# Sample states loaded ahead of the second output weights, sample rows' products and turns placed elsewhere, and the first weight block in two transfers

## The chip, the cores and the metric

One NeuronCore of a Trainium2 chip runs the kernel. The metric is device microseconds of one execution. Before the change the median of three runs is 1743.33 us (1741.56 to 1744.11).

## The reference

One step of a one-layer decoder runs for a prompt (512 rows of width 1024) and a sample group (8 sequences of 4 new rows, so 32 rows), with the same weights:

```python
h = rmsnorm(x);  hq|hf|hi|hg|mq|mk|mv = h @ w_in          # 7 blocks of 512 columns
HGRN2 (4 heads of 128): S_t = diag(f_t) S_{t-1} + k_t i_t^T;  o_t = S_t^T q_t
MoBA (8 heads of 64): attention over blocks of keys
x += concat(HGRN2 out, MoBA out) @ w_out                  # halves o0, o1
x += cross_attention(rmsnorm(x)) @ w_xo                   # queries: w_xq, halves xq0, xq1
x += hierarchical_moe(rmsnorm(x))                         # 2 of 32 experts for each row
y = rmsnorm(x)
```

The sample group starts from `state_hgrn` (8 x 4 states of 128 x 128, 2 MB) and reads paged keys and values; its new states are an output.

## The kernel before, in words

All data is f32. The rows stand in five tiles: tiles 0 to 3 of 128 prompt rows, and tile 4 (`NT`) of the 32 sample rows. Each engine has its own program, written in order by hand; they meet at semaphores.

Weights come in blocks of 1024 x 512 (2 MB), sent by SyncE (`weights`, line 612) into two slots in turn. A block goes only when the product that last reads the slot's earlier block is done (`last`, line 568). SyncE's program is one list (from line 640): the key pages and value pages of the sample batches (`key_pages(b)`, `value_pages(b)`, four transfers of 256 KB each), `o1` (line 643), the memory values, `xq0` to `xo1` (line 663), then the expert weights (lines 672 and 676 wait before the first of these). POOL has a queue of its own: constants, the sample states (line 757, into the tile `r_x`), their write-back after the update (line 763), the reload of x into the same place (line 766) and the memory keys.

Products are put in a ring of seven PSUM banks in the order of `plan_jobs` (line 122). A job names the engine that empties its bank (A is ScalarE, V is VectorE), and each engine must take its jobs in this order. TensorE waits for a bank through `J.wait_free`, for a copy through `J.wait_emptied`.

The steps that matter, in order of time:

- **Start.** Each tile is normed (ScalarE squares and roots at lines 839 and 841, VectorE scales at line 1299), turned by TensorE (`turn`, line 1961) and multiplied by block `mk` (`key_rows`, line 2025, products at line 2001). For a prompt tile a product is a loop over 8 blocks of 128 rows of the weights, two passes each.
- **Sample states.** After the last value product of the prompt (line 2139), TensorE waits at line 2182 for the states, multiplies by them (lines 2185 and 2188) and makes the updates (line 2198); VectorE adds them (line 1562).
- **Output projection.** `rows_summed(half, i)` is tile i by `o0` or `o1`. These products stand between the turning of the sample keys and the sample scores. For tile 4 the product is 64 small passes for each half (`quarters`, line 1974). VectorE adds the result to x (`add_rows`, line 1606, and line 1610 for tile 4).
- **Second norm and turn.** When both halves of a tile are added, ScalarE takes its root (`cross_norm_root`), VectorE scales it (`cross_norm`) and TensorE turns it (`cross_turn`). `X1_HALF` (line 115) is the order of the tiles. Tile 4 needs the sample outputs turned (`out_turned(1)`, copied by VectorE).
- **Queries.** `features_out("xq", half)` (line 1978) first multiplies the sample rows (line 1974), then makes four chunks of 128 features for all prompt rows (line 1989) and turns the sample rows' result (line 1992).

Then come cross-attention, its output, the router and the experts, whose 384 MB of weights pass through the same memory.

Of the kernel before, what the change touches and what calls it, by code (L numbers as in the profile page):

```python
# [28 lines left out]
KC = D // P  # L29
SEQ = 512  # L30
NT = SEQ // P
# [80 lines left out]


LAST_HALF = [NT] + list(range(NT))
X1_HALF = [0, 1, NT, 2, 3]

BANKS = (0, 1, 2, 3, 4, 5, 7)
RING = len(BANKS)
# [3 lines left out]
def plan_jobs():  # L122
# [3 lines left out]
    def add(eng, *name):  # L126
        jobs.append((name, eng))

    def turned(what, tiles):
        for i, _ in tiles:  # L130
            add("A", what, i, 0)
            add("V", what, i, 1)
# [85 lines left out]
    add("A", "Os", 1)  # L218
    turned("h2T", [(0, 0)])
    add("V", "OsT", 1)  # L220
    add("V", "x1", 0, NT)
    add("V", "x1", 1, NT)
    turned("h2T", [(1, 0)])
    add("V", "x1", 1, 2)
    turned("h2T", [(NT, 0)])
    add("V", "x1", 1, 3)
    turned("h2T", [(2, 0)])
    turned("h2T", [(3, 0)])

    def summed(what, turn, samples):  # L230
# [17 lines left out]
        for name in logit[NT:]:  # L248
            add("V", *name)

    for half in range(2):
        add("A", "xq", half, "rows")
        for c in range(5):
            add("AV"[c % 2], "xq", half, c)
    for h in range(XH + 1):
        if h < XH:
            for i in range(2):
# [79 lines left out]
def step_kernel(nc, a):  # L337

    with ExitStack() as ctx:
# [3 lines left out]
        def sem(name):  # L343
            return ctx.enter_context(nc.semaphore(name))
# [156 lines left out]
        const_in = sem("const_in")  # L501
        ident_in = sem("ident_in")
        w_in = [sem(f"wslot{n}_in") for n in range(2)]
        mem_in = sem("mem_in")
        s0_in = sem("s0_in")
        k_in = [sem(f"k{n}_in") for n in range(3)]
# [57 lines left out]
        def tok(i):  # L564
            return slice(P * i, P * i + rows(i))
# [2 lines left out]
        last = {"hf": ("hf", 4), "hq": ("hq", 4), "mk": ("mk", 4), "mq": ("mq", 4), "mv": ("mv", 4),  # L568
                "hi": ("hi", 4), "hg": ("hg", 4)}
        for n in range(2):  # L570
            last[f"o{n}"] = ("x1", n, (NT, LAST_HALF[-1])[n])
            last[f"xk{n}"] = ("mem", n, 1)
            last[f"xv{n}"] = ("mem", 2 + n, 1)
            last[f"xq{n}"] = ("xq", n, 4)
            last[f"xo{n}"] = ("x2", n, (NT, LAST_HALF[-1])[n])
# [30 lines left out]
        def _(sp):  # L606
# [5 lines left out]
            def weights(tag):  # L612
                n = WPOS[tag]
                name, col, _ = WBLOCKS[n]
                if n >= 2:
                    J.wait_filled(sp, *last[WBLOCKS[n - 2][2]])
                src = a[name][0].rearrange("(k p) n -> p k n", p=P)[:, :, 512 * col:512 * (col + 1)]
                sp.dma_start(wslot[n % 2], src).then_inc(w_in[n % 2], 16)

            def value_pages(*batches):  # L620
                for b in batches:
                    load_pages(sp, pages, vbuf[b % 4], "cache_moba_v", b, v_in)
# [6 lines left out]
            def key_pages(b):  # L629
                load_pages(sp, pages, kbuf[b % 3], "cache_moba_k", b, k_in[b % 3])  # L630
# [9 lines left out]
            sp.wait_ge(qx_done, 1)  # L640
            J.wait_filled(sp, "S", MB - 1, NT - 1)
            key_pages(1)
            weights("o1")
            value_pages(3)
            J.wait_filled(sp, "OT", 3)
            sp.wait_ge(out_mv, 32)
            key_pages(2)
            sp.wait_ge(out_memk[1], 16)
            value_pages(2)
            J.wait_filled(sp, "KT", 0, 3)  # L650
# [5 lines left out]
            for b in (5, 6, 7):  # L656
                J.wait_filled(sp, "KT", b - 3, 3)
                key_pages(b)
            J.wait_filled(sp, "Os", 0)
            value_pages(4, 5, 6, 7)  # L660
            J.wait_filled(sp, "Os", 1)
# [171 lines left out]
        def _(act):  # L833
# [24 lines left out]
            def turned(what, i):  # L858
                evac(hT[:, 0:4, tok(i)], what, i, 0,
                     view=lambda s: s.rearrange("p (k t) -> p k t", k=4)[:, :, 0:rows(i)])  # L860
# [244 lines left out]
                J.wait_filled(act, "h2T", X1_HALF[n - 2], 1)  # L1105
                cross_norm_root(n)
            turned("h2T", X1_HALF[3])
            turned("h2T", X1_HALF[4])

            def scaled_q(half, c):  # L1110
                J.wait_filled(act, "xq", half, c)
# [5 lines left out]
                                         s[:, 0:128].rearrange("p (c t) -> p c t", c=4), ACT.Copy, scale=XD ** -0.5)  # L1117
                J.empties(ins, "xq", half, c)

            for half in range(2):  # L1120
                sample_rows("xq", half)
                for c in (0, 2, 4):
                    scaled_q(half, c)

            for h in range(XH + 1):
                if h < XH:
# [148 lines left out]
        def _(dve):  # L1275
# [395 lines left out]
            turned("h2T", 0)  # L1671
            cross_norm(1)
            out_turned(1)
            add_rows("x1", 0, NT)
            add_rows("x1", 1, NT)
            turned("h2T", 1)
            cross_norm(2)
            add_rows("x1", 1, 2)
            turned("h2T", NT)
            cross_norm(3)  # L1680
            add_rows("x1", 1, 3)
            turned("h2T", 2)
            cross_norm(4)
            turned("h2T", 3)
            for half in range(2):
                for c in (1, 3):
                    J.wait_filled(dve, "xq", half, c)
                    J.empties(dve.tensor_scalar(qT[:, 4 * half + c, 0:SEQ], J.bank("xq", half, c), XD ** -0.5, None,
                                                ALU.mult), "xq", half, c)

            for h in range(XH + 1):
                if h < XH:
# [258 lines left out]
        def _(pe):  # L1951
# [23 lines left out]
                                        start=(k == 0), stop=(k == KC - 1), skip_group_check=True)  # L1975
                return ins

            def features_out(what, *key, chunks=range(5)):

                w = weights(what if not key else f"xq{key[0]}")  # L1980
                for c in chunks:
                    if c == 0:
                        J.wait_free(pe, what, *key, "rows")
                        J.fills(quarters(J.bank(what, *key, "rows"), NT, w, hT), what, *key, "rows")
                    J.wait_free(pe, what, *key, c)
                    s = J.bank(what, *key, c)
                    if c < 4:
                        for k in range(KC):
                            ins = pe.matmul(s, w[:, k, P * c:P * (c + 1)], hT[:, k, 0:SEQ], start=(k == 0), stop=(k == KC - 1))  # L1989
                    else:  # L1990
                        J.wait_emptied(pe, what, *key, "rows")
                        ins = pe.transpose(s[:, 0:P], srows[:, :], ident[:, :])
                    J.fills(ins, what, *key, c)

            def rows_of(name, i, w, lhs):
                J.wait_free(pe, *name)
                if i == NT:
                    J.fills(quarters(J.bank(*name), i, w, lhs), *name)
                    return
                for k in range(KC):  # L2000
                    ins = pe.matmul(J.bank(*name), lhs[:, k, tok(i)], w[:, k, :], start=(k == 0), stop=(k == KC - 1))  # L2001
                J.fills(ins, *name)

# [21 lines left out]
            def key_rows(i):  # L2025
                J.wait_emptied(pe, "hT", i, 0)
                J.wait_emptied(pe, "hT", i, 1)
                if i == 0:
                    weights("mk")
                rows_of(("mk", i), i, w, hT)  # L2030

            for i, r in TILES:
# [267 lines left out]
            sample_out(1)  # L2300
            cross_turn(0)
            out_turned(1)
            J.wait_emptied(pe, "hgT", NT)
            J.wait_emptied(pe, "OsT", 1)
            rows_summed(0, NT)
            rows_summed(1, NT)
            cross_turn(1)
            rows_summed(1, 2)
            cross_turn(2)
            rows_summed(1, 3)  # L2310
            cross_turn(3)
            cross_turn(4)

            def summed(what, wtag, lhs, turned, n0, meanwhile, samples, logit=None):

# [17 lines left out]
                if logit:  # L2333
                    logit(NT)

            J.wait_emptied(pe, "h2T", X1_HALF[-1], 0)
            J.wait_emptied(pe, "h2T", X1_HALF[-1], 1)
            for half in range(2):
                features_out("xq", half)

            for c in range(5):
                J.wait_emptied(pe, "xq", 1, c)
# [245 lines left out]
```

## Time and profile before

| | us |
|---|---|
| median of three runs | 1743.33 |
| the profiled execution | 1745.59 |
| its span, first to last instruction | 1743.4 |
| TensorE busy in it | 1453.9 (83%) |
| VectorE busy | 503.1 (29%) |
| ScalarE busy | 271.9 (16%) |
| DMA, mean rate | 299 GB/s |

A busy share is a mean over stages with different limits. To value a change in one stage one reads there which engine stood still, for how long, and what ended the wait. The chain that ended last is followed back from the last instruction, each step to what released it. In a timeline, the bracket at the end of a line is the idle time of the engine just before it and what ended it.

### The profile page before, as it was taken

How to read it: one execution, taken by the hardware profiler on the slowest of the kernel's cores; microseconds unless marked ns; L12 is line 12 of the kernel's file. 1: busy time of each engine (PE TensorE's matmuls, PEld its weight loads, DVE VectorE, ACT ScalarE, POOL GpSimd, SP SyncE). 2: the span in 40 equal slices, each digit the busy share in tenths (PEclk: the TensorE clock that was granted, in tenths of full speed). 3: DMA queues.
4: the chain of work that ended last, by engine and by line, in shares of the span. 5: the costliest groups of instructions: out<-in, count | busy, mean ns of one | idle time of the engine just before them, and what ended most of it. 6: DMA issues, size and time to landing. Idle time of an engine off the chain costs nothing.

```text
span 1743.4 us, 17609 instructions
## 1 busy us (share of the span) xinstructions
PE 1453.9 (83%) x6988; PEld 644.6 (37%) x6988; DVE 503.1 (29%) x929; ACT 271.9 (16%) x594; POOL 96.9 (6%) x108
## 2 busy tenths in 40 slices
PE   6999999879989999869778877877887788788781
PEld 3444554444454564523222322322232223223220
DVE  2056775453230331432121211112121211112124
ACT  3114234432210220200000000000000000000002
POOL 3100000000000000000000000000000000000002
PEclk9999999989989999979989989988998998899895
DMA  8931220476361256459999999999999999999974
GB/s 298 278 122 48 77 95 15 156 267 237 121 254 49 72 218 246 160 224 428 427 427 427 430 427 428 428 427 427 428 429 426 428 426 428 428 428 428 422 315 175
DMA packets 76085, 521.99 MB, mean 299 GB/s; under 512 B 8466, under 2 KB 9026, under 8 KB 51456
## 3 DMA queue, kind: packets, MB, share of 16 engines
q1 hardware_dynamic: 58112, 468.47, 65.4%
q0 software_dynamic: 14800, 45.98, 7.9%
q10 hardware_dynamic: 3120, 6.82, 1.0%
q8 instruction: 36, 0.59, 0.1%
q14 instruction: 17, 0.14, 0.0%
HBM read 496.98 MB, written 32.11 MB: 303 GB/s over the span
## 4 chain that ended last, share of the span: by engine, by line
PE 48%; DMA 40%; DVE 7%; ACT 2%; issue 2%; SPq 1%; POOL 0%; POOLq 0%; ACTq 0%; DVEq 0%
DMA ring<-w 39%; PE psum L2533 12%; PE psum L2001 10%; PE psum L1989 7%; PE psum L2091 3%; PE psum L2510 3%; PE psum L1974 1%; PE psum L2218 1%; PE psum L2366 1%; PE psum L2389 1%; DVE ring L1417 1%; PE psum L2351 1%; DMA ring<-w_in 1%; PE psum L2206 1%; PE psum L1961 1%
## 5 line engine op out<-in xcount | busy, mean ns | idle before, releaser
L2510 PE MATMUL psum<-ring,r_c 128*64 128x512 f32 x1536 | 368.9, 636 | 84.6 <-DMA ring<-w 83.7
L2533 PE MATMUL psum<-ring,r_c 128*64 128x512 f32 x1024 | 260.8, 663 | 90.3 <-DMA ring<-w 78.6
L2510 PEld LDWEIGHTS psum<-ring,r_c 128*64 128x64 f32 x1536 | 120.1, 147 | 329.9 <-issue 212.1
L1904 DVE TENSOR_SCALAR r_c<-r_c 128x512 f32<-128x512 f32 x32 | 13.7, 427 | 751.3 <-ACT r_c L1208 751.3
L2533 PEld LDWEIGHTS psum<-ring,r_c 128*64 128x64 f32 x1024 | 82.4, 151 | 246.5 <-issue 204.0
L1989 PE MATMUL psum<-r_h,ring 128*128 128x512 f32 x320 | 138.8, 594 | 0.0
L2001 PE MATMUL psum<-ring,r_h 128*128 128x512 f32 x256 | 114.6, 607 | 4.6 <-DMA ring<-w_in 4.6
L1906 DVE RECIPROCAL r_c<-r_c 128x512 f32<-128x512 f32 x32 | 107.3, 3353 | 1.1
L1208 ACT ACTIVATE r_c<-psum 128x512 f32<-128x512 f32 x32 | 19.1, 597 | 540.4 <-PE psum L2510 540.4
L1989 PEld LDWEIGHTS psum<-r_h,ring 128*128 128x128 f32 x320 | 60.6, 191 | 75.3 <-issue 75.3
L809 POOL DMA_INDIRECT out_rows<-r_c,maskd x32 | 31.6, 988 | 897.7 <-ACT r_c L1218 865.4
L2001 PEld LDWEIGHTS psum<-ring,r_h 128*128 128x128 f32 x256 | 49.3, 195 | 65.0 <-issue 64.7
L1218 ACT ACTIVATE r_c<-psum 128x512 f32<-128x512 f32 x32 | 19.1, 597 | 334.2 <-PE psum L2533 334.2
L2510 PE MATMUL psum<-r_h,r_c 128*64 128x512 f32 x256 | 57.6, 592 | 0.0
L2510 PE MATMUL psum<-r_mix,r_c 128*64 128x512 f32 x256 | 57.6, 592 | 0.0
L2091 PE MATMUL psum<-ring,r_h 128*128 128x512 f32 x128 | 57.0, 598 | 0.6 <-DVE r_x L1470 0.6
L2001 PE MATMUL psum<-ring,r_mix 128*128 128x512 f32 x128 | 56.8, 597 | 0.9 <-ACT r_mix L852 0.9
L2001 PE MATMUL psum<-ring,r_c 128*128 128x512 f32 x128 | 56.1, 595 | 0.0
L1606 DVE TENSOR_TENSOR r_x<-r_x,psum 128x512 f32<-128x512 f32 x16 | 11.0, 687 | 95.5 <-PE psum L2001 83.7
L852 ACT ACTIVATE ring<-psum 128x512 f32<-128x512 f32 (+3 forms) x63 | 28.0, 531 | 64.8 <-PE psum L2001 26.1
L2091 PEld LDWEIGHTS psum<-ring,r_h 128*128 128x128 f32 x128 | 23.7, 190 | 31.0 <-issue 30.7
L2001 PEld LDWEIGHTS psum<-ring,r_c 128*128 128x128 f32 x128 | 23.9, 190 | 29.3 <-issue 29.3
(350 smaller groups left out, 1295.4 us busy)
## 6 DMA issues: line engine op xcount, KB each, us to landing
ring<-w SPq DMA_DIRECT2D x160, 2048.0 KB, 22.2
r_h<-w SPq DMA_DIRECT2D x16, 2048.0 KB, 28.2
r_mix<-w SPq DMA_DIRECT2D x16, 2048.0 KB, 29.9
ring<-w_in SPq DMA_DIRECT2D x7, 2048.0 KB, 14.1
out_rows<-zeros POOLq DMA_DIRECT2D x3, 4096.0 KB, 21.6
ring<-cache_mem_v SPq DMA_DIRECT2D x8, 1024.0 KB, 9.4
ring<-cache_mem_k POOLq DMA_DIRECT2D x8, 1024.0 KB, 7.7
ring<-cache_moba_v SPq DMA_DIRECT2D x24, 256.0 KB, 7.1
```

The costliest lines, as they stand in the source:

```text
L809: pool.indirect_dma_start(half_rows, bass.IndirectOffsetOnAxis(ap=sidx[:, e:e + 1], axis=0), ys[e % 2], None, bounds_check=2 * NE * CAP - ...
L852: J.empties(act.activation(out, view(src) if view else src, ACT.Copy), *name)
L1208: act.activation(he[u], psum[2 + 2 * u], ACT.Exp, scale=-1.0).then_inc(up_exp, 1)
L1218: act.activation(ys[u], psum[7], ACT.Copy).then_inc(y_free, 1)
L1417: v(dve.reciprocal(g, g))
L1906: dve.reciprocal(he[u], he[u]).then_inc(dve_moe, 1)
L1961: ins = pe.transpose(s[:, P * k:P * k + r], src[0:r, P * (4 * half + k):P * (4 * half + k + 1)], ident[0:r, 0:r])
L1989: ins = pe.matmul(s, w[:, k, P * c:P * (c + 1)], hT[:, k, 0:SEQ], start=(k == 0), stop=(k == KC - 1))
L2001: ins = pe.matmul(J.bank(*name), lhs[:, k, tok(i)], w[:, k, :], start=(k == 0), stop=(k == KC - 1))
L2091: ins = pe.matmul(J.bank("mem", n, i), memT[:, k, P * i:P * (i + 1)], w[:, k, :], start=(k == 0), stop=(k == KC - 1))
L2510: ins = pe.matmul(psum[2 + 2 * u + m][CAP * half:CAP * (half + 1), :], xT[:, k, CAP * u:CAP * (u + 1)], moe_place(2 * q + m, u)[:, kk, 512 ...
L2533: ins = pe.matmul(psum[7][CAP * half:CAP * (half + 1), :], heT[u][:, k % 4, CAP * (k // 4):CAP * (k // 4 + 1)], moe_place(4 + q, u)[:, kk, ...
```

## The change

First block: `mk` is sent as two transfers, of its first and last four row blocks. The first product waits for the first alone, and for the second before its fifth row block.

Loads: `o1` moves from behind the key pages of batch 1 to behind those of batch 6. The value pages of batch 3 move behind the key pages of batch 2, and SyncE waits for the sample states before it sends them.

Rows: tile 4 becomes the last of `X1_HALF`. The product of tile 2 by `o1` and the turn of tile 1 go ahead of tile 4's product by `o0`, that of tile 3 behind it, and tile 4's product by `o1` goes between the turns of tiles 2 and 3. Tile 4's turn goes behind the second chunk of the first query block, and its query product from the head of this block to just ahead of the fourth chunk. The other engines' lists follow the same order.

```diff
-X1_HALF = [0, 1, NT, 2, 3]
+X1_HALF = [0, 1, 2, 3, NT]
...
-            last[f"o{n}"] = ("x1", n, (NT, LAST_HALF[-1])[n])
+            last[f"o{n}"] = ("x1", n, NT)
...
+                if tag == "mk":
+                    sp.dma_start(wslot[n % 2][:, 0:KC // 2, :], src[:, 0:KC // 2, :]).then_inc(w_first_in, 16)
+                    sp.dma_start(wslot[n % 2][:, KC // 2:, :], src[:, KC // 2:, :]).then_inc(w_in[n % 2], 16)
+                    return
...
             key_pages(1)
-            weights("o1")
-            value_pages(3)
             J.wait_filled(sp, "OT", 3)
             sp.wait_ge(out_mv, 32)
             key_pages(2)
+            sp.wait_ge(s0_in, 16)
+            value_pages(3)
...
                 key_pages(b)
+                if b == 6:
+                    weights("o1")
...
+            scaled_q(0, 0)
+            turned("h2T", NT)
+            scaled_q(0, 2)
+            sample_rows("xq", 0)
+            scaled_q(0, 4)
+            sample_rows("xq", 1)
+            for c in (0, 2, 4):
+                scaled_q(1, c)
...
-            add_rows("x1", 0, NT)
-            add_rows("x1", 1, NT)
+            add_rows("x1", 1, 2)
             turned("h2T", 1)
             cross_norm(2)
-            add_rows("x1", 1, 2)
-            turned("h2T", NT)
-            cross_norm(3)
+            add_rows("x1", 0, NT)
             add_rows("x1", 1, 3)
             turned("h2T", 2)
+            cross_norm(3)
+            add_rows("x1", 1, NT)
+            turned("h2T", 3)
             cross_norm(4)
-            turned("h2T", 3)
...
+                    if half == 0 and c == 1:
+                        turned("h2T", NT)
...
+                    if name == ("mk", 0) and k == KC // 2:
+                        weights("mk")
...
                 if i == 0:
-                    weights("mk")
+                    pe.wait_ge(w_first_in, 16)
...
+            rows_summed(1, 2)
+            cross_turn(1)
             J.wait_emptied(pe, "hgT", NT)
             J.wait_emptied(pe, "OsT", 1)
             rows_summed(0, NT)
+            rows_summed(1, 3)
+            cross_turn(2)
             rows_summed(1, NT)
-            cross_turn(1)
-            rows_summed(1, 2)
-            cross_turn(2)
-            rows_summed(1, 3)
             cross_turn(3)
-            cross_turn(4)
...
-            for half in range(2):
-                features_out("xq", half)
+            features_out("xq", 0, chunks=(0, 1), rows_at=None)
+            cross_turn(4)
+            features_out("xq", 0, chunks=(2,), rows_at=None)
+            J.wait_emptied(pe, "h2T", NT, 0)
+            J.wait_emptied(pe, "h2T", NT, 1)
+            features_out("xq", 0, chunks=(3, 4), rows_at=3)
+            features_out("xq", 1)
```

## Rows read from the trace of the kernel before

**Rows 1.** The page's chain that ended last, by engine and by line.

```profile
PE 48%; DMA 40%; DVE 7%; ACT 2%; issue 2%; SPq 1%; POOL 0%; POOLq 0%; ACTq 0%; DVEq 0%
DMA ring<-w 39%; PE psum L2533 12%; PE psum L2001 10%; PE psum L1989 7%; PE psum L2091 3%; PE psum L2510 3%; PE psum L1974 1%; PE psum L2218 1%; PE psum L2366 1%; PE psum L2389 1%; DVE ring L1417 1%; PE psum L2351 1%; DMA ring<-w_in 1%; PE psum L2206 1%; PE psum L1961 1%
```

**Rows 2.** A wait of SyncE's queue: total us, times, longest us.

```profile
SPq L672 <- PE psum L2407: 18.4, 1, 18.4
```

**Rows 3.** Timeline of the start, TensorE: start us, us, engine, line.

```profile
17.84 8.53 PE L2001 MATMUL psum<-ring,r_h 128*128 128x512 f32 x16 [4.58 <-DMA ring<-w_in]
```

**Rows 4.** Timeline around the sample states: SyncE's and POOL's issues, then TensorE.

```profile
363.42 0.40 SPq L618 DMA_DIRECT2D ring<-w_out  x1
373.57 1.88 SPq L603 DMA_DIRECT2D ring<-cache_moba_k  x4
...
366.62 1.74 POOL L757 DMA_DIRECT2D r_x<-state_hgrn  x1 [296.37 <-PE psum L2154]
...
371.03 2.37 PE L2139 MATMUL psum<-ring 128*64 128x512 f32 x16 [1.89 <-ACT ring L852]
383.04 0.77 PE L2185 MATMUL psum<-ring,atts 128*128 128x128 f32 x2 [9.63 <-issue]
```

**Rows 5.** End of the projection: chain, TensorE, and stretches (length, busy times, PEclk, DMA, GB/s).

```profile
486.14 3.51 issue
...
515.74 1.97 PE L1961 MATMUL psum<-ident,r_c 128*128 128x128 f32 x8 [3.28 <-DVE r_c L1299]
550.04 1.95 PE L1974 MATMUL psum<-ring,r_h 128*32 128x128 f32 x64
...
489.60:496.00 6.40, 6.35 (x129) 6.19 (x129) 1.13 (x4) 0.00 (x0) 0.00 (x0) 0.56 1.02 412
518.50:522.20 3.70, 3.67 (x65) 3.31 (x65) 0.00 (x0) 0.00 (x0) 0.00 (x0) 0.50 0.42 162
```

**Rows 6.** SyncE's DMA queue in 0:12, 12:15, 15:18: packets, MB, share.

```profile
q1 hardware_dynamic: 1009, 3.25, 81.2%
...
q1 hardware_dynamic: 563, 1.15, 104.5%
...
q1 hardware_dynamic: 359, 0.70, 64.4%
```

**Rows 7.** POOL's DMA queue in 371:372, then 374:378; the states' landing (us).

```profile
q0 software_dynamic: 7, 0.03, 7.0%
...
q0 software_dynamic: 222, 0.91, 66.8%
...
r_x<-state_hgrn POOLq DMA_DIRECT2D x1, 2048.0 KB, 16.3
```

**Rows 8.** Timeline: reload of x (VectorE), keys 6 (SyncE), first product by o1 (TensorE).

```profile
409.25 0.69 DVE L1606 TENSOR_TENSOR r_x<-r_x,psum 128x512 f32<-128x512 f32 x1 [11.76 <-DMA r_x<-x_prompt]
...
422.67 1.88 SPq L603 DMA_DIRECT2D r_h<-cache_moba_k  x4
...
465.47 7.13 PE L2001 MATMUL psum<-ring,r_mix 128*128 128x512 f32 x16
```

**Rows 9.** Timeline of VectorE and ScalarE: sample rows' add, tile 3's norm, a turn emptied.

```profile
493.35 1.17 DVE L1610 TENSOR_TENSOR r_x<-r_x,psum 32x128 f32<-32x128 f32 x4 [3.80 <-PE psum L1974]
511.62 0.69 DVE L1606 TENSOR_TENSOR r_x<-r_x,psum 128x512 f32<-128x512 f32 x1 [3.61 <-PE psum L2001]
514.40 1.28 DVE L1299 SCALAR_TENSOR_TENSOR r_c<-r_x,nt,gain 128x1024 f32<-128x1024 f32 x1
...
512.40 1.06 ACT L839 ACTIVATE r_c<-r_x 128x1024 f32<-128x1024 f32 x1 [6.12 <-DVE r_x L1606]
516.89 0.60 ACT L852 ACTIVATE r_h<-psum 128x512 f32<-128x512 f32 x1 [2.62 <-PE psum L1961]
```

**Rows 10.** Issue and landing of the query weights (two transfers), SyncE.

```profile
493.34 18.64 SPq L618 DMA_DIRECT2D ring<-w_xq  x2
...
DMA to landing us min/median/max: 8.1/12.0/15.8
```

More of the change, by code:

```diff
@@ L220, in plan_jobs @@
     add("V", "OsT", 1)
+    add("V", "x1", 1, 2)
+    turned("h2T", [(1, 0)])
     add("V", "x1", 0, NT)
[L222 to L225, printed above, removed]
     add("V", "x1", 1, 3)
     turned("h2T", [(2, 0)])
+    add("V", "x1", 1, NT)
     turned("h2T", [(3, 0)])
@@ L249, in summed @@
             add("V", *name)
-    for half in range(2):
-        add("A", "xq", half, "rows")
-        for c in range(5):
-            add("AV"[c % 2], "xq", half, c)
+    add("A", "xq", 0, 0)
+    add("V", "xq", 0, 1)
+    turned("h2T", [(NT, 0)])
+    add("A", "xq", 0, 2)
+    add("A", "xq", 0, "rows")
+    add("V", "xq", 0, 3)
+    add("A", "xq", 0, 4)
+    add("A", "xq", 1, "rows")
+    for c in range(5):
+        add("AV"[c % 2], "xq", 1, c)
     for h in range(XH + 1):
@@ L503, in step_kernel @@
         w_in = [sem(f"wslot{n}_in") for n in range(2)]
+        w_first_in = sem("first_half_of_mk_in")
         mem_in = sem("mem_in")
@@ L1107, in _ @@
             turned("h2T", X1_HALF[3])
-            turned("h2T", X1_HALF[4])
             def scaled_q(half, c):
@@ L1118, in scaled_q @@
                 J.empties(ins, "xq", half, c)
[L1120 to L1123, printed above, removed]
+            scaled_q(0, 0)
[6 more added lines that the diff above has]
+                scaled_q(1, c)
             for h in range(XH + 1):
@@ L1976, in quarters, with features_out @@
                 return ins
-            def features_out(what, *key, chunks=range(5)):
+            def features_out(what, *key, chunks=range(5), rows_at=0):
                 w = weights(what if not key else f"xq{key[0]}")
                 for c in chunks:
-                    if c == 0:
+                    if c == rows_at:
                         J.wait_free(pe, what, *key, "rows")
@@ L2334, in summed @@
                     logit(NT)
-            J.wait_emptied(pe, "h2T", X1_HALF[-1], 0)
-            J.wait_emptied(pe, "h2T", X1_HALF[-1], 1)
-            for half in range(2):
-                features_out("xq", half)
+            J.wait_emptied(pe, "h2T", NT - 1, 0)
+            J.wait_emptied(pe, "h2T", NT - 1, 1)
+            features_out("xq", 0, chunks=(0, 1), rows_at=None)
[5 more added lines that the diff above has]
+            features_out("xq", 1)
             for c in range(5):
```

## The prediction

> **What bounds the kernel now.** I read the chain that ended last first. TensorE holds 48% of the span and DMA 40%, nearly all of the latter expert weights [rows 1]. So there are two halves: up to about 760 us a chain of TensorE products, and after it a stream of expert weights. All that the change touches lies in the first half. What is saved there reaches the end if the stream's start follows the chain: SyncE waits 18.4 us for the products at line 2407 before it sends the first expert weights (line 672) [rows 2]. It is a queue that waits for slots, so an earlier chain starts it earlier. I count a us before 660 as a us at the end.
>
> In the first half I looked for places where TensorE stands still on the chain. Three lie in the change's path: 4.58 us before the first product, which waits for the block mk [rows 3]; 9.63 us at 373.4 to 383.0, which the chain calls issue, but the next instruction reads r_x and line 2182 waits for the sample states [rows 4]; and the end of the first output projection, with idle stretches of 3.51 and 3.28 us and slow products behind both: the granted clock is 0.56 (mostly the 1.2 GHz level) at 489.6 to 496 and 0.50 at 518.5 to 522.2 [rows 5].
>
> **Part 1: block mk in two transfers.** Nothing is removed; SyncE issues one transfer more (about 0.4 us of its time) and the first product waits for 1.05 MB instead of 2.10 MB. Ahead of mk in its queue lie four prompt tiles, a gain and the sample rows, 2.75 MB together. The queue had moved 3.25 MB by 12 us, so 0.50 MB of mk, and 1.15 MB more from 12 to 15 us [rows 6], 0.383 MB a us. The first half has passed at 12 + 0.55 / 0.383 = 13.4. The full block has passed at about 16.9 (0.45 MB after 15 at the 0.23 MB a us left beside the constants, 0.70 MB in 3 us [rows 6]), and its product began at 17.84, so 0.9 later; the first then begins at 14.3 to 14.5. Gain 3.4 us. Half of the first tile's sixteen passes takes 4.3 us, so the second half, due at 17.9, is there when wanted. Bounds: all of the 4.58 us, or 1.5 us if the second transfer's packets mix with the first's. The loads behind it keep their order, and block hf moves already while mk's products run. The tiles that follow are TensorE work without a gap, so the gain stays.
>
> What speaks against it: here the queue moves block mk at 0.383 MB a us, with six smaller transfers ahead of it. The Trainium skill (DMA: Bandwidth & Descriptors, Bandwidth) gives 6.15 us for 1 MB alone and asks for batches of at least 1 MiB; two such in a row would take 12.3 us, land the second half near 23 us, and make this gain about zero.
>
> **Part 2: the states ahead of o1.** Before, SyncE issues o1 (2.10 MB, 363.42) and behind it value pages (1.05 MB) just ahead of the states' transfer on POOL (366.62) [rows 4]. In 371 to 372 the states' queue q0 has moved only 7 packets [rows 7]: it got nothing until the 3.15 MB before it had passed. Then the key pages of 373.57 took part of the rest: from 374 to 378 q0 moved 0.91 MB with 66.8% of the engines' time [rows 7]. The states landed after 16.3 us [rows 7].
>
> After, only the key pages of batch 1 precede, which SyncE sends before o1, and they are through. Scaled to all engines, q0's rate is 0.91 / 4 / 0.668 = 0.34 MB a us. From the end of the POOL instruction (366.62 + 1.74 = 368.4) 2.10 MB take 6.2 us; the 0.26 MB of hg_prompt that ACT sends meanwhile add 0.8; the key pages of 373.57 come in for the last us. I take TensorE's start as 376.2. Its own ready time is 371.03 + 2.37 = 373.4 [rows 4]. Gain 383.04 - 376.2 = 6.8 us. Bounds: 9.6 (landing hidden), and 2.3, where q0 starts as late as before (371.5) and moves at 0.23 MB a us as it did beside q1 (9.2 us, landing 380.7).
>
> By the fit of the Trainium skill (DMA: Bandwidth & Descriptors, Anatomy of one DMA), 2.0 us and bytes at 436 GB/s, the states would land after an estimated 6.8 us, at 373.4: the gain would be 9.6 and the sum 20.3.
>
> What the added wait holds up: behind SyncE's wait for the states stand the value pages 3 and 2 and the keys 3 to 7. The first 12 issues take 5.6 us of SyncE (1.88 for four [rows 4]), and keys 3 are wanted after tile 1's product of the output projection. The backlog of value pages shares the engines with the states' write-back and the reload of x, whose first part VectorE awaits at 409.25 (11.76 us idle [rows 8]); a later landing costs VectorE first, and TensorE needs what follows it only behind a further 7 us product. I cost it at nothing; without that cover it is the delay itself, an estimated 1 to 3 us for 1.05 MB more at 0.34 MB a us. o1 is now sent behind keys 6, which went at 422.67, and is wanted at 465.47 [rows 8]: 41 us of cover for 3 MB. Its cost is nothing.
>
> **Part 3: sample rows moved.** After the turn of the sample outputs ends at 486.14, TensorE waited for VectorE's copies (3.51 us) and did both sample products at the low clock, 6.4 us [rows 5]. In the new order it goes on with tile 2: product 7.03, turn of tile 1 1.0, sample product of the first half 1.95 (the price at the high clock [rows 5]), product of tile 3 7.03: at 503.1. The copies are done long before. Now the chain is tile 3's norm: from the start of its add at 511.62 to the end of its scaling, 514.40 + 1.28, is 4.1 us in the old order [rows 9]; so it ends at 507.3. TensorE fills 1.0 (turn of tile 2) and 1.95 (second sample product) and then waits a little over 1 us. VectorE then adds the sample rows, 1.17; ACT does their square and root, about 1.4 (its square alone 1.06), and only then empties tile 3's turn, 0.60 [rows 9]. So the query products start at 507.3 + 1.2 + 1.4 + 0.6 = 510.5. What is late next is that ACT norm.
>
> Before, these products began at 522.2, with the sample rows' product (3.67 at the low clock) done. Now that product and the turn of the sample rows (0.7) fall inside the query stage at the high clock: 1.95 + 0.7. I also charge 1.7 us of low clock behind the new gap, as behind the old one (3.67 against 1.95 [rows 5]). Gain 522.2 - 510.5 - 2.65 - 1.7 = 7.3 us. Bounds: 9.0 if the clock stays up, 4.0 if the query weights come late: they are now released by the first sample product at 496.1 instead of 493.3, and before they landed after 15.8 us [rows 10], at 509.1. The engines were full of memory keys and values then, so I expect the same landing; at worst 511.9, with as much again lost to the clock.
>
> **Sum.** 3.4 + 6.8 + 7.3 = 17.5 us. The profiled execution took 1745.6 us (span 1743.4 and 2.2 around it), 2.3 above the median of the runs, 1743.3; taking the 17.5 off its own time gives 1728.1, and off the median 1725.8, which is my forecast. The bounds together give 7.8 to 23.2, so 1720 to 1735.5.
>
> **Rivals.**
> - The states' transfer is slow by itself (its rows are 512 bytes long). For it: q0 moved no more than 0.23 MB a us in this stretch; against it: it had q1 and hg_prompt beside it. 368.4 + 9.2 and 1.7 for the same company give a landing at 379.3, a gain of 3.7, a total of 1728.9. Chance 0.15.
> - Covers hold better: the states land before TensorE is ready, and the clock stays up. By the idle time in the rows: 3.4 + 9.6 + 9.0 = 22.0, total 1721.3. For it: before, the states had o1 ahead of them. Against: q0's measured rate. Chance 0.10. The fit of the Trainium skill (DMA: Bandwidth & Descriptors, Anatomy of one DMA) would act like this.
> - A weight block comes late: either mk's halves mix or slow each other (gain 0 of 3.4), or the query weights land 2.8 later (3.3 lost). Total 1729.1. For it: q1 and q0 share the engines then; against: both were limited by total bandwidth. Chance 0.08. [...]
> - Nothing reaches the end: the expert stream keeps its own start. Total 1743.3. Against: the wait of [rows 2], for a product of the chain. Chance 0.04.
> - Slower: o1 becomes the wait at its first product. It is now sent about 41 us before it is due [rows 8], and nothing is sent ahead in its place. Each us beyond 41 from issue to landing is a us of waiting; past 41 + 17.5 = 58.5 us the kernel is slower, and at 64 us the total is 1743.3 - 17.5 + 23 = 1749. Against: the query weights, with 6 MB beside them, needed 15.8 us [rows 10]. Chance 0.03.
>
> **How the numbers follow.** The forecast holds 0.60. Three other faster cases hold 0.33 and lie at 1721 to 1729. The range 1719 to 1733.5 takes these with their bounds; the far end of the sum of all low bounds and the last two rivals are left out. About 0.2% (3.5 us) is what a measurement can tell from no change: faster by more than that 0.93, within it 0.04, slower 0.03.
>
> **What would show it.** In the changed profile: the first product near 14.5; states landing in 8 to 10 us and idle time ahead of line 2185 of under 4 us; no idle stretch before the sample products, whose time is half; a short gap before tile 3's turn, and the first query product about 12 us earlier than the earlier gains alone put it; expert weights sent 17 us sooner. The forecast is wrong if the states' transfer still takes over 12 us, if line 2001 waits for the second half of mk, or if the query products wait for their weights.

## The result, and the profile after

The changed kernel takes 1729.38 us (median of 4 runs, 1724.6 to 1730.4), the kernel before 1743.72 (4 runs beside it, 1741.56 to 1744.43): a ratio of 0.9914, 95% interval 0.9893 to 0.9935, so 14.3 us less. The forecast was 1725.8 with a range of 1719 to 1733.5. One execution of a run further down (tile 3's turn emptied first) took 2980.56 us and is left out of its ratio. The profiled executions differ by 15.1 us (spans of 1743.4 and 1728.3). Their timelines can be laid side by side and say where the time went:

| place on TensorE | before | after | earlier by | of it new, and forecast |
|---|---|---|---|---|
| start of the first product | 17.84 | 14.39 | 3.45 | |
| start of the second product | 27.08 | 24.29 | 2.79 | |
| product of values ahead of the states | 371.03 | 368.42 | 2.61 | part 1: 2.6 (3.4) |
| first product with the states | 383.04 | 375.60 | 7.44 | |
| first product of the output projection | 399.39 | 391.62 | 7.77 | part 2: 5.2 (6.8) |
| first scores after the queries | 580.73 | 565.19 | 15.54 | part 3: 7.8 (7.3) |
| first expert product | 760.97 | 745.43 | 15.54 | |
| end of the span | 1743.4 | 1728.3 | 15.1 | sum: 15.5 (17.5) |

SyncE's wait ahead of the first expert weights is as long as before (18.4 us in [rows 2]), and their first transfers go out 15.55 us earlier, so the stream of expert weights did start with the chain and kept the gain. The wait in the changed kernel, then SyncE's issue in the kernel before and in the changed one:

```profile
SPq L684 <- PE psum L2429: 18.5, 1, 18.5
...
659.79 2.29 SPq L672 DMA_DIRECT2D ring<-w  x4
...
644.24 2.14 SPq L684 DMA_DIRECT2D ring<-w  x4
```

**The start.** The timeline of the changed kernel's TensorE, against [rows 3]: start us, us, engine, line, in brackets the idle time ahead and what ended it.

```profile
14.39 9.19 PE L2019 MATMUL psum<-ring,r_h 128*128 128x512 f32 x16 [1.04 <-DMA ring<-w_in]
...
24.29 7.03 PE L2019 MATMUL psum<-ring,r_h 128*128 128x512 f32 x16
```

The idle stretch is 1.04 us instead of 4.58. The product itself takes 9.19 us instead of 8.53, so 0.7 of the 3.45 is gone before the second product. That is a difference between these two executions and no price of the split (Part 1 further down). Its weight loads show how (the same timeline, TensorE's weight loads): the first come 0.85 us apart, the later ones 0.43, half as far.

```profile
16.23 0.34 PEld L2019 LDWEIGHTS psum<-ring,r_h 128*128 128x128 f32 x1 [0.52 <-issue]
17.09 0.34 PEld L2019 LDWEIGHTS psum<-ring,r_h 128*128 128x128 f32 x1 [0.52 <-issue]
...
19.12 0.19 PEld L2019 LDWEIGHTS psum<-ring,r_h 128*128 128x128 f32 x1 [0.24 <-issue]
19.55 0.19 PEld L2019 LDWEIGHTS psum<-ring,r_h 128*128 128x128 f32 x1 [0.24 <-issue]
```

**The states.** POOL's issue, its landing (the list of DMA issues) and TensorE's timeline, against [rows 4] and [rows 7]:

```profile
363.99 1.74 POOL L769 DMA_DIRECT2D r_x<-state_hgrn  x1 [291.48 <-PE psum L2172]
...
r_x<-state_hgrn POOLq DMA_DIRECT2D x1, 2048.0 KB, 11.5
...
368.42 2.37 PE L2157 MATMUL psum<-ring 128*64 128x512 f32 x16 [1.90 <-ACT ring L864]
375.60 0.77 PE L2203 MATMUL psum<-ring,atts 128*128 128x128 f32 x2 [4.81 <-issue]
```

The landing takes 11.5 us instead of 16.3, and the idle stretch ahead of the product is 4.81 instead of 9.63. The queues say what is left of it. In 366 to 368, 368 to 372 and 372 to 374 (packets, MB, share of 16 engines):

```profile
q0 software_dynamic: 45, 0.18, 57.6%
q10 hardware_dynamic: 343, 0.17, 29.8%
...
q0 software_dynamic: 299, 1.22, 101.1%
...
q0 software_dynamic: 142, 0.58, 102.8%
```

POOL's queue begins about 2.8 us after the issue, as ACT's hg_prompt (q10) ends, and then moves 1.22 MB in 4 us and 0.58 MB in 2 us, 0.29 to 0.31 MB a us, with the engines full and nothing beside it. The granted clock (the third number from the end of each row) falls in the gap and stays at 0.50, the 1.2 GHz level, for the 4 us behind it:

```profile
374.00:376.00 2.00, 0.40 (x2) 0.43 (x2) 2.00 (x4) 0.00 (x0) 0.00 (x0) 0.50 1.00 346
376.00:378.00 2.00, 2.00 (x34) 1.65 (x37) 0.11 (x1) 0.00 (x0) 0.00 (x0) 0.50 1.05 387
378.00:380.00 2.00, 2.00 (x43) 1.51 (x32) 0.00 (x0) 0.00 (x0) 0.00 (x0) 0.50 1.06 387
```

**The sample rows.** TensorE's timeline from the first sample product on, then ScalarE's, and the stretch 502 to 510, against [rows 5] and [rows 9]:

```profile
485.97 1.95 PE L1990 MATMUL psum<-ring,r_mix 128*32 128x128 f32 x64
...
495.79 1.95 PE L1990 MATMUL psum<-ring,r_mix 128*32 128x128 f32 x64
499.15 1.09 PE L1977 MATMUL psum<-ident,r_c 128*128 128x128 f32 x8 [1.40 <-DVE r_c L1314]
502.18 15.70 PE L2005 MATMUL psum<-r_h,ring 128*128 128x512 f32 x32 [1.93 <-ACT r_h L864]
...
500.26 1.05 ACT L851 ACTIVATE r_c<-r_x 32x1024 f32<-32x1024 f32 x1 [2.59 <-PE psum L1977]
...
501.55 0.57 ACT L864 ACTIVATE r_h<-psum 128x512 f32<-128x512 f32 x1
...
502.00:510.00 8.00, 7.82 (x15) 3.36 (x16) 1.43 (x3) 0.12 (x1) 0.55 (x1) 0.79 0.62 224
```

The gaps of 3.51 and 3.28 us and the two sample products at the low clock are gone. In their place stand 1.40 us for tile 3's norm and 1.93 us for ScalarE, which squares the sample rows (500.26) before it empties tile 3's turn (501.55). Behind that the granted clock is 0.79 on average for 8 us: the first two query chunks take 15.70 us.

### The profile page after: what moved, and what is told of

It is laid out like the page before. It is cut to its first block, busy times and chain, and to the rows that moved or that the text cites. A ratio compares the mean times of both kernels' runs of the same rounds, so it can differ in the third digit from the quotient of the medians.

```text
span 1728.3 us, 17613 instructions
## 1 busy us (share of the span) xinstructions
PE 1451.4 (84%) x6988; PEld 638.0 (37%) x6988; DVE 502.8 (29%) x929; ACT 272.3 (16%) x594; POOL 97.3 (6%) x108
## 4 chain that ended last, share of the span: by engine, by line
PE 48%; DMA 40%; DVE 7%; ACT 2%; issue 1%; SPq 1%; POOL 0%; POOLq 0%; ACTq 0%; DVEq 0%
DMA ring<-w 39%; PE psum L2555 12%; PE psum L2019 10%; PE psum L2005 7%; PE psum L2109 3%; PE psum L2532 3%; PE psum L1990 1%; PE psum L2236 1%; PE psum L2388 1%; PE psum L2411 1%; DVE ring L1432 1%; PE psum L2373 1%; PE psum L1977 1%; PE psum L2157 1%; PE psum L2399 1%
```

## The experiments

A single run can't carry differences of 2 us here: executions of the kernel before lay between 1741.4 and 1752.6 on one chip, with granted clocks of 0.929 to 0.919. So each run is read by its trace first, at the place that its edit touches, and by its ratio second.

**One part at a time.** The kernel before, with one of the three parts each. Block mk in two transfers:

```diff
+                if tag == "mk":
+                    sp.dma_start(wslot[n % 2][:, 0:KC // 2, :], src[:, 0:KC // 2, :]).then_inc(w_first_in, 16)
+                    sp.dma_start(wslot[n % 2][:, KC // 2:, :], src[:, KC // 2:, :]).then_inc(w_in[n % 2], 16)
+                    return
...
```

> The kernel before, with the first weight block in two transfers and nothing else. Theory (three parts that add up): the first product begins at 14.4 us instead of 17.84, the second at 24.3 instead of 27.1, everything behind it 2.8 us earlier up to the wait for the sample states, the total 2.8 us below the kernel before. Rival (the later stages take it back, since the loads behind block mk or the states' transfer keep their own times): the total moves by under 1 us, and the idle time ahead of the product by the states grows by 2 to 3 us.

Measured: ratio 0.996 (0.9943 to 0.9977). The first product's row of its timeline:

```profile
14.45 9.28 PE L2008 MATMUL psum<-ring,r_h 128*128 128x512 f32 x16 [1.07 <-DMA ring<-w_in]
```

The second product begins at 24.44 instead of 27.08, 2.6 us earlier: part 1 as in the whole change. The idle stretch at the states stays (10.16 us). This trace doesn't show the lead any further on: its execution ran at a mean granted clock of 0.922, and the product of values ahead of the states came at 371.71, before at 371.03. That the lead reaches the end rests on the ratio and on the whole change.

The order of the loads:

```diff
-            weights("o1")
-            value_pages(3)
             J.wait_filled(sp, "OT", 3)
             sp.wait_ge(out_mv, 32)
             key_pages(2)
+            sp.wait_ge(s0_in, 16)
+            value_pages(3)
...
+                if b == 6:
+                    weights("o1")
```

> The kernel before, with the order of SyncE's loads changed alone (o1 behind the key pages of batch 6, the value pages of batch 3 behind a wait for the states). Theory: the states land 11 to 12 us after their issue instead of 16.3, the idle time ahead of the product by the states falls from 9.63 to 4.8 us, the total by 5 us. Rival (the loads put later cost something where they land): the states land as early, but VectorE waits longer for the reloaded rows of x and TensorE for its copies, and the total falls by 3 us or less.

Measured: ratio 0.9956 (0.994 to 0.9971). TensorE's timeline and the landing:

```profile
379.66 0.77 PE L2187 MATMUL psum<-ring,atts 128*128 128x128 f32 x2 [4.82 <-issue]
...
r_x<-state_hgrn POOLq DMA_DIRECT2D x1, 2048.0 KB, 11.5
```

The idle stretch and the landing are those of the whole change, to 0.01 us: part 2 owes nothing to the others.

The sample rows (the order on VectorE and TensorE; ScalarE's list goes with them):

```diff
             out_turned(1)
-            add_rows("x1", 0, NT)
-            add_rows("x1", 1, NT)
+            add_rows("x1", 1, 2)
             turned("h2T", 1)
...
+            rows_summed(1, 2)
+            cross_turn(1)
             J.wait_emptied(pe, "hgT", NT)
...
```

> The kernel before, with the sample rows' products and turns moved alone. Theory: no idle stretch of 3.5 us ahead of the sample products, each of which takes 1.95 us instead of 3.2; the query stage ends 7.7 us earlier, and so does the kernel. Rival (the moved products only fill time that the clock gives back in any order): the stretch of idle and low clock reappears ahead of the query products, and the total falls by 4 us or less.

Measured: ratio 0.9962 (0.9943 to 0.9981). Its first sample product and its first query chunks:

```profile
494.58 1.95 PE L1983 MATMUL psum<-ring,r_mix 128*32 128x128 f32 x64
...
510.78 16.77 PE L1998 MATMUL psum<-r_h,ring 128*128 128x512 f32 x32 [1.93 <-ACT r_h L857]
```

From the product with the states to the scores it takes 191.0 us, before 197.7: 6.7 us saved, and its two chunks took 1.07 us more than those of the whole change behind the same wait of 1.93, which makes up the difference to 7.8. By the traces the parts add up: 2.6 + 5.2 + 6.7 is 14.5. The three ratios would add to 1.2%, 21 us, with an uncertainty of about 3 us each; the interval of the split alone, 4 to 10 us, doesn't even hold its 2.6. I go by the traces, since executions differ by so much; why the ratios add to more isn't shown.

**Which of the loads held the states up?** Only o1 moved (the value pages wait for the product that o1 waited for, so that they go at the time they went):

```diff
-            weights("o1")
+            J.wait_filled(sp, *last["xv1"])
             value_pages(3)
...
+                if b == 6:
+                    weights("o1")
```

> The kernel before, with o1 alone moved behind the key pages of batch 6; the value pages of batch 3 stay where they were (with the wait for the last memory value product, which o1's own issue held before) and SyncE does not wait for the states. Theory A (the states wait for what was sent before them, 3.15 MB, of which o1 is two thirds, and then move at their own rate of 0.29 MB a us): the states' first packets come at 369 us, they share the engines with key pages and value pages only at the end, the idle time ahead of the product by the states is 5 to 6 us and the total falls by 4 to 5 us, nearly all that the second part gives. Theory B (the value pages, sent beside the states, take as much of the engines as o1 did): idle 7 us or more, the total falls by 1 to 2.5 us.

and only the value pages moved, with o1 in its old place:

```diff
             weights("o1")
-            value_pages(3)
...
+            sp.wait_ge(s0_in, 16)
+            value_pages(3)
```

> The kernel before, with o1 in its old place; only the value pages of batch 3 move behind a wait for the states. Theory A (the states wait until what was sent before them has passed, and o1's 2.1 MB are most of that): from the states' issue to the product that reads them 14.5 to 16 us (16.4 before, 11.6 in the changed kernel, 12.6 with o1 alone moved). Theory B (the pages that share the engines with the states cost most): 12 to 13 us.

POOL's issue and the product with the states, in the first of the two and in the second:

```profile
372.90 1.74 POOL L759 DMA_DIRECT2D r_x<-state_hgrn  x1 [301.61 <-PE psum L2156]
...
385.52 0.77 PE L2187 MATMUL psum<-ring,atts 128*128 128x128 f32 x2 [4.84 <-issue]
```

```profile
364.70 1.74 POOL L758 DMA_DIRECT2D r_x<-state_hgrn  x1 [293.78 <-PE psum L2155]
...
378.79 0.76 PE L2186 MATMUL psum<-ring,atts 128*128 128x128 f32 x2 [7.29 <-issue]
```

From issue to product: 16.4 us before, 12.6 with o1 moved (ratio 0.9962, 0.9946 to 0.9979), 14.1 with the pages moved (one run, 1738.08), 11.6 with both. So o1 alone takes 3.8 of the 4.8 us off and the pages alone 2.3; together they are worth less than the two added. The first is on Theory A's side; with the pages moved, 14.1 lies between the two theories' ranges, so the pages count for more than Theory A had them. The product ahead of the gap ran slower in the first of them (3.36 us instead of 2.37), so its idle stretch of 4.84 flatters it by 1.

**Is the rest of the landing the transfer's own?** The changed kernel with the states sent by SyncE instead of POOL:

```diff
             key_pages(1)
+            J.wait_filled(sp, "o", NT - 1)
+            J.wait_emptied(sp, "U", NCH - 1)
+            sp.dma_start(s0, a["state_hgrn"][0].rearrange("b h k v -> k b h v")).then_inc(s0_in, 16)
...
-            pool.dma_start(s0, a["state_hgrn"][0].rearrange("b h k v -> k b h v")).then_inc(s0_in, 16)
```

> The changed kernel, with the states' transfer sent by SyncE at the same point instead of by POOL. Theory R (rows of 512 bytes limit the transfer to 0.29 MB a us, whoever sends it): the rate stays at 0.28 to 0.30 MB a us, the landing comes 9 to 10.5 us after the issue instead of 11.5, because the first packet comes sooner, and the idle time ahead of the product falls from 4.8 to 2.8 to 3.8 us. Theory S (POOL's software queue limits it): 0.38 to 0.40 MB a us, landing after 7 to 8 us, idle time under 1.5 us.

Measured: ratio 0.9901 (0.9876 to 0.9927), and the product later after the issue, 12.8 us instead of 11.6:

```profile
363.79 0.89 SPq L655 DMA_DIRECT2D r_x<-state_hgrn  x1
...
376.59 0.77 PE L2205 MATMUL psum<-ring,atts 128*128 128x128 f32 x2 [5.79 <-issue]
```

Neither theory, as written: the edit had moved something else. POOL's next transfer, 0.5 MB of the cross norm's gain, no longer stood behind the states on POOL's queue and went ahead of them. The gain's first bytes came at about 365.2, the states' at about 366.9, though SyncE had issued the states 0.2 us earlier. The queues in 366 to 368:

```profile
q0 software_dynamic: 96, 0.34, 64.6%
q1 hardware_dynamic: 49, 0.10, 15.2%
```

So once more, with that gain held until the states are there:

```diff
+            pool.wait_ge(s0_in, 16)
             pool.dma_start(gain[:, :], a["g_cross"].to_broadcast([P, D])).then_inc(gain_in, 16)
```

> The changed kernel with the states sent by SyncE's queue, and GpSimd's load of the cross norm's gain held until they have landed, so that nothing new goes ahead of them. Theory S (it was the gain that held the states up when SyncE sent them: issue 363.8, first packets about 367, product 12.8 us after the issue): the states' bytes begin to move by 366.5, their product comes 9.5 to 11 us after the issue, and the idle stretch ahead of it is 2 to 4 us instead of 4.81; the time 1 to 3 us below the changed kernel's, ratio to the kernel before about 0.990. Theory R (2 MB in rows of this length take about 11.5 us beside the key loads whoever sends them): 11.5 us or more, idle stretch 4.5 to 6, ratio as the changed kernel's.

Measured: ratio 0.9913 (0.9893 to 0.9932). SyncE's issue, TensorE's timeline, and SyncE's queue in 365 to 367:

```profile
362.93 0.88 SPq L655 DMA_DIRECT2D r_x<-state_hgrn  x1
...
367.56 3.35 PE L2160 MATMUL psum<-ring 128*64 128x512 f32 x16 [1.89 <-ACT ring L867]
...
373.06 0.76 PE L2206 MATMUL psum<-ring,atts 128*128 128x128 f32 x2 [2.15 <-issue]
...
q1 hardware_dynamic: 272, 0.56, 95.4%
```

Theory S holds: the bytes move from about 364.6 (1.7 us after the issue), the product comes 10.1 us after the issue, and the idle stretch is 2.15 us. The rate is 0.28 MB a us over these two, about as on POOL's queue: that part hardly depends on the sender. Why it is below the 0.383 of block mk [rows 6] no run here separates; rows of 512 bytes are one reading. Still the run is no faster than the changed kernel. The product ahead of the gap took 3.35 us instead of 2.37, and more of what follows the gap ran at the low clock: from the start of that product to the first product of the output projection it is 22.11 us, in the changed kernel 391.62 - 368.42 = 23.20 (and 24.36 in its second profile, below, where the product ahead of the gap was as slow). Of 2.66 us of idle time 1.1 reached the chain against the first of these profiles and 2.25 against the second, too little for a ratio to show.

**What stands behind the wait of 1.93 us?** The changed kernel with ScalarE emptying tile 3's turn ahead of the sample rows' norm:

```diff
+                if n == 4:
+                    turned("h2T", X1_HALF[3])
...
-            turned("h2T", X1_HALF[3])
```

> The changed kernel, with ScalarE emptying tile 3's turn ahead of the sample rows' square and root instead of behind them. Theory (that norm of the sample rows is what the first query product waits for): the query products start 1.2 us sooner after tile 3's turn (idle 0.8 instead of 1.93), and if the shorter stop keeps the clock up, their first two chunks take 13.9 instead of 15.7 us: 1.2 to 3 us in all. Rival (VectorE's add and copy, or the query weights, land as late): idle time above 1.6 us, nothing gained.

Measured: ratio 0.9881 (0.9855 to 0.9907; three executions). The wait falls to 1.30 us and has a new cause, the query weights:

```profile
506.85 13.97 PE L2006 MATMUL psum<-r_h,ring 128*128 128x512 f32 x32 [1.30 <-DMA ring<-w_xq]
```

From the first sample product to the scores it is 76.85 us, in the changed kernel 79.22. Of these 2.4 us 0.63 are the wait; the chunks' 1.73 are the clock, and the run with the states first had chunks of 14.00 us behind the full wait of 1.93. So 1.7 of the 2.4 aren't this edit's for certain. Both edits so far together (SyncE's states, gain not held):

> The changed kernel with both edits (states sent by SyncE, tile 3's turn emptied first). Theory: the two gains add up, 2 to 5 us below the changed kernel, so 1725 us less 2 to 5 on a chip where the changed kernel takes its 14 us less than the kernel before. Rival (one stop is replaced by the next on the same chain): 1 us or less.

Measured: ratio 0.9912 (0.9892 to 0.9932), 6.05 us idle at the states, 1.44 on the query weights and chunks of 15.37: no gain that can be measured. Then the query weights ahead of the memory values on SyncE:

```diff
-            mem_values(range(3))
-            for tag in ("xq0", "xq1", "xo0", "xo1"):
+            for tag in ("xq0", "xq1"):
+                weights(tag)
+            mem_values(range(3))
+            for tag in ("xo0", "xo1"):
```

> The changed kernel with ScalarE emptying the third tile's turn ahead of the sample rows' norm (the run before that did this had a wait of 1.30 us on the query weights ahead of the query products, and 13.97 us for the first two chunks), and with SyncE sending the two blocks of query weights ahead of the three loads of memory values (3 MB). Theory A (the query weights land late because 3 MB of memory values go ahead of them on the same queue): the weights land before the last turn is emptied, the wait ahead of the query products is named by an engine's copy and is 0.7 to 1.0 us, the first two chunks take 13.9 to 14.5 us, and the stage is 0.3 to 0.6 us shorter than in that run, 2.5 to 3 us shorter than in the changed kernel. Theory B (the 3 MB of memory keys on GpSimd's queue hold them as much): the wait is still named by the weights and is 1.2 us or more. Either way the memory values, sent later, are not waited for. Ratio to the kernel before 0.989 to 0.991.

Measured: ratio 0.9903 (0.9888 to 0.9918). SyncE's issue and the query products:

```profile
489.09 10.16 SPq L628 DMA_DIRECT2D ring<-w_xq  x2
...
502.13 13.97 PE L2008 MATMUL psum<-r_h,ring 128*128 128x512 f32 x32 [0.83 <-ACT r_h L866]
```

Theory A holds: the weights land after about 8 us instead of 11, the wait is a copy's again, 0.83 us, and from the first sample product to the scores it is 76.39 us, 2.8 less than in the changed kernel, 0.5 less than with ScalarE's edit alone. The memory values are not waited for.

**All of it together**, the states by SyncE with the gain behind them and the two edits at the query products:

> All of it together: the states by SyncE with the gain behind them, the third tile's turn first, the query weights ahead of the memory values. If both theories named first hold, the gains add: 1 to 3 us at the states and 2.5 to 3 us at the query products, ratio to the kernel before 0.987 to 0.989, faster than the changed kernel by about 4 us. If the states' product is not earlier (Theory R), about 2.5 us, 0.989 to 0.990. If the clock gives it back, 0.991.

Measured: 1725.55 us (median of 5 runs), ratio 0.9885 (0.9867 to 0.9903). TensorE's timeline at the start, at the states and at the queries:

```profile
14.48 7.11 PE L2025 MATMUL psum<-ring,r_h 128*128 128x512 f32 x16 [1.42 <-DMA ring<-w_in]
...
371.77 0.77 PE L2209 MATMUL psum<-ring,atts 128*128 128x128 f32 x2 [2.09 <-issue]
...
497.94 13.97 PE L2011 MATMUL psum<-r_h,ring 128*128 128x512 f32 x32 [0.83 <-ACT r_h L869]
```

Both gains stand in one trace: 1.1 us at the states (22.09 over the same stretch, against the changed kernel's first profile) and 2.8 at the queries (76.39). The first product at 7.11 us, which no edit touched, gave this execution 2 us more. It is also the one product that waited for the second half of mk: its weight loads, 0.43 us apart, are held up by 0.33 us at the fifth row block.

```profile
17.13 0.19 PEld L2025 LDWEIGHTS psum<-ring,r_h 128*128 128x128 f32 x1 [0.24 <-issue]
17.89 0.30 PEld L2025 LDWEIGHTS psum<-ring,r_h 128*128 128x128 f32 x2 [0.57 <-DMA ring<-w_in]
```

The changed kernel, run again to weigh those 2 us:

> The changed kernel once more, unchanged, with more runs than the four it was judged by. Two readings of the run of everything together (ratio 0.9885, with the first product at 7.11 us and the first two query chunks at 13.97): if its 4 us over the changed kernel are its own, this run gives 0.990 to 0.993 and a median of 1728 to 1732; if they are mostly the granted clock of those executions, this run may come to 0.988 to 0.990 as well. The first product of its profiled execution takes anything from 8.5 to 10.2 us, and the first two query chunks 14.0 or 15.4 to 15.7 behind the same wait of 1.93 us: the stretch from the first sample product to the scores is 77.5 or 79.2 us, by the clock alone.

Measured: 1729.7 us (median of 4), ratio 0.9906 (0.9889 to 0.9922), 16.5 us below the kernel before beside it, with the wait of 1.93 and chunks of 15.70 us again. The version with everything is the best of all by its median, 4 us below the changed kernel's, and 3.9 by the two stretches. The two intervals still overlap, and 1.7 of those us are query chunks at the high clock: they took 13.97 in all three runs with a wait of 1.30 us or less, and 15.70 in three with 1.93 (16.77 and 14.00 in two others).

## Why the prediction was right, and where it was off

The direction, the three places and the range held. Two of the signs named ahead did not come: the states landed after 11.5 us, not 8 to 10, and the idle time ahead of their product was 4.81 us, not under 4. The forecast was 3.6 us too low: 2.0 from the three terms (17.5 forecast, 15.5 in the chain), 0.4 given back in the expert stream (15.1 at the end), 0.8 between these two executions and the medians (14.3), and 0.4 because the kernel before came out at 1743.7 beside it, not at 1743.3.

- **Part 1, 3.4 forecast, 2.6 between the two profiles.** The landing was right: first product forecast for 14.3 to 14.5, measured 14.39. In the changed kernel no pass waited for the second half; in the one execution that made its first passes at full pace, it held them up by 0.33 us, at 17.89, where the forecast had it due. Assumed without saying so was that the product keeps its 8.53 us. Its first passes go at half pace for a number that differs from execution to execution: 8.52 to 10.15 us in eight of the nine traces with the split, 7.11 in the ninth, 8.53 to 9.96 in the five without. The profile before is the quickest of those five, so its pair shows too little: the second product begins at 24.05 on average in the nine, at 27.88 in the five, 3.8 us earlier. The 3.4 was not too much. The Trainium skill (DMA: Bandwidth & Descriptors, Bandwidth) gives 6.15 us for 1 MB; an estimated 12.3 us for two in a row would have made this gain zero. The trace disagrees, with 3.5 us less to wait. The Trainium skill's batch size of at least 1 MiB (the same section) is no ground against the split: half a block is 1.05 MB and meets it.
- **Part 2, 6.8 forecast, 5.2 measured.** The cause was right: o1 and the pages stood ahead of the states (the runs with one of the two moved). Mis-sized were two terms of the 9.6 us that I counted from issue to product; it was 11.6. The bytes began 2.8 us after the issue, not 1.7, and moved at 0.29 to 0.31 MB a us, not at the 0.34 that I had scaled up from a stretch in which the queue held 66.8% of the engines' time. With 2.10 MB the rate alone is 6.8 to 7.2 us against 6.2. The 1.6 us that I added for hg_prompt and the key pages came out in size only, by luck: hg_prompt was through when the states began, and by 374.0, 1.6 us ahead of the product, all but 0.12 MB had moved. The rival of a transfer that is slow by itself, at 0.23, was half right: on POOL's queue the engines are full at 0.29 with nothing beside it. From the product of values to the output projection the traces give 23.2 to 24.4 us with the loads moved and the states on POOL's queue (five) and 28.4 to 29.0 with the old order (three), 4.9 by the means: this is the term that was forecast too high. The estimated 6.8 us of the Trainium skill (DMA: Bandwidth & Descriptors, Anatomy of one DMA) is not borne out: 11.5.
- **What the loads held up: nothing, as forecast.** SyncE waited 2.7 us for the states. VectorE's wait for x grew from 11.76 us [rows 8] to 12.90 without reaching TensorE. o1 went out at 416.83, its first product began at 457.63 with no idle time ahead of it.
- **Part 3, 7.3 forecast, 7.8 measured.** The steps came out: the sample products at 1.95 us; the wait for tile 3's norm, "a little over 1 us", 1.40; ScalarE's norm of the sample rows as what is late next. That the 1.7 us charged for the low clock behind it were met (15.70 against 13.97, 1.73) has luck in it: behind the same wait the two chunks took anything from 14.00 to 16.77. From the output projection to the scores five traces with the old order took 177.5 to 181.5 us, five with the new one and nothing else changed at the queries 171.9 to 174.7, 7.6 by the means. The query products were forecast for 510.5 in the time of the kernel before; they came at 502.18 + 7.77 = 509.95. The rival of late query weights was not it, but stood right behind: with ScalarE's delay taken away, they were the wait. The low bound of 4.0 has a slip: 1.4 us late and as much again to the clock leave 4.5.

By these means the three parts are worth 3.8 + 4.9 + 7.6 = 16.3 us, and the changed kernel came out 14.3 us below the kernel before by its first four executions and 16.5 by the other four. The forecast of 17.5 is then high by about 1.2, and the states' transfer (1.9 too high) more than accounts for that.

## What to carry to other kernels

A transfer that the chain waits for is freed by sending what is not yet due after it, on every queue: what was sent 3 us earlier on another queue delayed it by about 5 us, and moving the transfer itself to another queue let a third transfer past it. Of an idle stretch taken off the chain, count only what the clock leaves: shortening a gap from 4.8 to 2.2 us gave 1.1 to 2.3, and one from 1.9 to 0.8 gave 1.1 and, in both runs that had it, the high clock behind it. Where executions differ by more than the gain, compare stretches of the timeline between two fixed products, and over several traces: the one profile before made part 1 look 1.2 us too small.

## What was not expected

- **The same wait, two outcomes.** The product of values ahead of the states follows a wait of 1.9 us in every trace; it took 2.37 us in most and 3.35 to 3.37 in four, the changed kernel's second profile among them, where the granted clock read 0.72 and then 0.50. The query chunks behind 1.93 us took 14.00, 15.70 or 16.77. Differences of this kind are how I read the spread of one kernel over 11 us; I have not added them up.
- **A clock row that is silent at the start.** Over the slow passes of the first product the granted clock reads 1.00 in the changed kernel's profile, though the loads are 0.85 us apart, then 0.43. In the run with the load order alone it reads 0.50 over such passes. That both are the same low clock is argued from the factor of two, not shown.
- **The order of issue is not the order of the bytes.** The gain load, issued 0.2 us after the states on another queue, had its first bytes about 1.7 us before them; in 366 to 368 it moved 0.34 MB while they moved 0.10, and it cost them 2.7 us.
